# From expert sums to output with tokens on partitions, and overflow rounds ahead of the main round

## The reference

```python
# first block, after its attention: x is (256, 1024)
hx2 = modulate(rmsnorm(x, norm2_g), sh2, sc2)
x = x + g2 * moe(hx2, ...)        # 32 experts, the 4 best of each token, hidden width 1024
x = rmsnorm(x, final_g)
# second block
h = rmsnorm_2(x, norm_mix_pre)
merged = ...                       # three attentions of h @ w_in, gated and summed
x = x + rmsnorm_2(merged @ w_out, norm_mix_post)
h = rmsnorm_2(x, norm_ffn_pre)
u = causal_depthwise_conv(h @ w_ffn_up, ...)          # 2 x 2816 channels
y = (gelu(u_gate) * u_val) @ w_ffn_down
x = x + rmsnorm_2(y, norm_ffn_post)
```

## Time and profile before

| what | us |
|---|---|
| median of 3 runs | 1701.89 |
| lowest and highest of them | 1701.84, 1705.04 |
| the profiled execution's own time | 1704.64 |
| its span in the profile | 1702.8 |
| PE busy in the span | 1586.2 |
| DVE, ACT busy | 542.3, 435.3 |

### The profile page before, as it was taken

How to read it: one execution, slowest core, us unless ns; L and a number is a source line. 1 busy time by engine, 2 the same in 40 slices (tenths; PEclk the granted TensorE clock), 3 DMA queues, 4 the chain that set the end, 5 groups by cost and what they waited for, 6 DMA issues and landing times.

```text
span 1702.8 us, 23717 instructions
## 1 busy us (share of the span) xinstructions
PE 1586.2 (93%) x10016; PEld 977.8 (57%) x10016; DVE 542.3 (32%) x1089; ACT 435.3 (26%) x849; POOL 7.2 (0%) x16
## 2 busy tenths in 40 slices
PE   5999999999999999999999999998699999899997
PEld 3786776443343333334333433333299988789997
DVE  3755513110101010110101010101255474477863
ACT  3433622010001010101101100000445552456542
POOL 0000000000000000000000000000000100000000
PEclk9999998999999999999999999999999999999999
DMA  9325736999999999999999999999734624425420
GB/s 393 152 80 221 294 119 250 433 431 432 432 431 431 431 431 431 431 433 434 433 433 432 433 431 432 431 432 431 299 116 157 186 99 149 149 99 198 175 99 25
DMA packets 27432, 524.79 MB, mean 308 GB/s; under 512 B 2931, under 2 KB 7027, under 8 KB 7492
## 3 DMA queue, kind: packets, MB, share of 16 engines
q1 hardware_dynamic: 24368, 519.06, 73.2%
q10 hardware_dynamic: 2484, 3.19, 0.7%
q0 software_dynamic: 512, 1.57, 0.4%
HBM read 522.72 MB, written 1.08 MB: 308 GB/s over the span
## 4 chain that ended last, share of the span: by engine, by line
PE 59%; DMA 34%; DVE 3%; ACT 2%; issue 1%; SPq 0%; ACTq 0%; DVEq 0%
PE ps L596 58%; DMA ring<-in_w_down 33%; PE ps L724 1%; DMA arena<-in_ctxT 1%; DMA ring<-in_first 1%; DVE ring_r L1641 0%; DVE arena L1623 0%; PE ps L1078 0%; DVE nrm L1620 0%; ACT w_high L1448 0%; DVE hx_lo L1648 0%; DVE arena L1654 0%; DVE arena L1955 0%; ACT L1191 0%; ACT arena L1198 0%
## 5 line engine op out<-in xcount | busy, mean ns | idle before, releaser
L596 PE MATMUL ps<-ring,arena 128*64 128x512 f32 (+1 forms) x3872 | 721.6, 532 | 45.4 <-DMA ring<-in_w_down 31.2
L596 PEld LDWEIGHTS ps<-ring,arena 128*64 128x64 f32 (+1 forms) x3872 | 240.3, 132 | 478.1 <-issue 403.4
L596 PE MATMUL ps<-arena_r,w_high 128*128 128x256 f32 x1840 | 339.5, 287 | 10.2 <-DVE arena_r L1935 9.4
L596 PEld LDWEIGHTS ps<-arena_r,w_high 128*128 128x128 f32 x1840 | 289.8, 193 | 15.0 <-issue 12.2
L596 PE MATMUL ps<-arena 128*128 128x128 f32 (+5 forms) x1780 | 262.4, 379 | 6.8 <-DVE arena L1838 1.6
L596 PE MATMUL ps<-arena_r,ring_r 128*128 128x256 f32 x920 | 261.7, 284 | 0.0
L1862 DVE TENSOR_SCALAR arena<-ps 128x512 f32<-128x512 f32 x32 | 22.1, 692 | 716.4 <-PE ps L596 716.4
L596 PEld LDWEIGHTS ps<-arena 64*128 64x128 f32 (+3 forms) x1780 | 167.5, 176 | 112.1 <-issue 98.1
L596 PEld LDWEIGHTS ps<-arena_r,ring_r 128*128 128x128 f32 x920 | 178.2, 194 | 0.0
L1909 DVE TENSOR_TENSOR ring_r<-ring,w_high 128x1024 fp32r<-128x1024 f32 x120 | 142.0, 1221 | 102.4 <-ACT w_high L1448 102.4
L1448 ACT ACTIVATE w_high<-ring 128x1024 fp32r<-128x1024 f32 x120 | 120.8, 1054 | 26.4 <-PE ps L596 26.4
(11 more groups left out here) (203 smaller groups left out, 1052.2 us busy)
## 6 DMA issues: line engine op xcount, KB each, us to landing
ring<-in_w_gate_up SPq DMA_DIRECT2D x64, 4096.0 KB, 20.8
ring<-in_w_down SPq DMA_DIRECT2D x32, 4096.0 KB, 19.7
ring<-in_second SPq DMA_DIRECT2D x32, 2048.0 KB, 8.2
ring<-in_first SPq DMA_DIRECT2D x19, 2048.0 KB, 12.5
ring<-in_first SPq DMA_DIRECT2D x3, 1024.0 KB, 5.1
ring<-in_second SPq DMA_DIRECT2D x2, 1024.0 KB, 5.0
small<-in_small ACTq DMA_DIRECT2D x1, 1024.5 KB, 8.3
arena<-in_xT SPq DMA_DIRECT2D x1, 1024.0 KB, 8.1
```

Of the source, the lines that this page charges most:

```text
L596: return nc.tensor.matmul(out_, lhsT, rhs, start=start, stop=stop, **kw)
```

## The change

- After the experts the residual is `x_tm`: 2 groups of 128 tokens on partitions, each with 1024 features. `combine` is 4 products of 128 tokens by 512 features; the residual itself is added by 16 products with the identity (`add_residual`) ahead of the last expert's down product.
- g2 is put on a row by 2 products of ones with a diagonal, and multiplied into `b_dn` once and into each expert's output by DVE (`scaled_down`), which takes the copy from ACT.
- `start_sums` becomes 4 products of 512 columns, all ahead of the branch and the first gather.
- Overflow rounds, with their branches, stand ahead of the main round on PE, ACT, DVE and SP.
- Norms take sums along a row (ACT's Square with an accumulator). The normed residual is turned back to features by products with a diagonal of the inverse roots (`turned`), from which ACT and DVE make the high and low parts.
- Output and down products have tokens as the stationary operand (128x128) and 512 weight columns as the moving one (`token_rows`); the last four down parts are done for token group 0 first and group 1 after it.
- Three rows of norm weights (512 KB each, repeated on all partitions) are loaded on ACT's queue. The output leaves in 4 writes of 256 KB.

```diff
-            stream(moe_units, 0, slot_full)
             sp.wait_ge(most_set, 1)
             count = sp.value_load(most_i[0:1, 0:1], min_val=0, max_val=T)
             with sp.If(count > SLOTS):
...
+            stream(moe_units, 0, slot_full)
...
+            pe.wait_ge(g2_set, 1)
+            for half in range(2):
+                mm(ps[:, 4 + half, :], ones[:], g2_diag[:, 4 * half:4 * half + 4].rearrange("p k n -> p (k n)"), True,
+                   True).then_inc(g2_mm, 1)
             sum_squares(NORM2, sq2, 2, T)
...
+            for bank in (6, 7, 5, 4):
+                t, half = (bank - 4) // 2, bank % 2
+                if bank == 4:
+                    pe.wait_ge(most_set, 1)
+                mm(ps[:, bank, :], gates_t[:, P * t:P * t + P], b_dn[0:N_EXPERTS, 512 * half:512 * half + 512], True, False,
+                   skip_group_check=True)
...
-                def combine():
-                    for c in range(4):
+                def combine(done):
+                    for t in range(TT):
                         for half in range(2):
-                            m = 4 * half + c
                             rows_ = slice(SLOTS * half, SLOTS * half + SLOTS)
-                            last = mm(ps[:, 4 + m // 2, T * (m % 2):T * (m % 2) + T], y_e[rows_, P * c:P * c + P],
-                                      sgt[rows_, :], False, False, skip_group_check=True)
+                            last = mm(ps[:, 4 + 2 * t + half, :], sgt[rows_, P * t:P * t + P], y_e[rows_, :], False, False,
+                                      skip_group_check=True)
+                        if done is not None:
+                            last.then_inc(done, 1)
                     return last
...
+                def add_residual():
+                    for t in range(TT):
+                        for k in range(KC):
+                            mm(ps[:, 4 + 2 * t + k // 4, P * (k % 4):P * (k % 4) + P], xT[:, k, P * t:P * t + P], ident,
+                               False, False, skip_group_check=True)
...
+                if S is MAIN:
+                    add_residual()
                 pe.wait_ge(S.at_ready, r * 32 + N_EXPERTS)
                 pe.wait_ge(S.sgt_ready, r * 33 + (N_EXPERTS + 1))
                 filled_pair(2, N_EXPERTS)
                 down(2, 0)
                 down(2, 1)
-                combined(N_EXPERTS - 1).then_inc(S.round_done, 1)
+                if S is MAIN:
+                    combined(N_EXPERTS - 1, x2_mm)
+                else:
+                    combined(N_EXPERTS - 1).then_inc(S.round_done, 1)
...
-            round_pe(MAIN, 0, start_sums)
             with if_more(pe):
...
+            round_pe(MAIN, 0)
+            def turned(x, t, k):
+                return mm(chunk_bank(k)[:, P * t:P * t + P], x[:, t, P * k:P * k + P], diag[:, t, :], True, True)
+            pe.wait_ge(diag_set, TT)
+            for k in range(KC):
+                if k >= 4:
+                    pe.wait_ge(h_lo_set, 2 * KC + k - 3)
+                for t in range(TT):
+                    last = turned(x_tm, t, k)
+                last.then_inc(turn_mm, 1)
...
+            def token_rows(n, t, bank, hi, lo, k, first, last):
+                tok = slice(P * t, P * t + P)
+                w_hi = part_hi(n)
+                w_lo = part_of(n, ring_r)
+                for x_, w, at_start, at_end in ((hi, w_hi, first, False), (lo, w_hi, False, False), (hi, w_lo, False, last)):
+                    for half in range(2):
+                        done_ = mm(ps[:, bank + half, :], x_[:, k, tok], row_of(w, half), at_start, at_end,
+                                   skip_group_check=True)
+                return done_
+            for k in range(KC):
+                n = 2 * J_OUT + k
+                pe.wait_ge(w_lo_set, N_PARTS1 + n + 1)
+                pe.wait_ge(mg_lo_set, k // 2 + 1)
+                for t in range(TT):
+                    last = token_rows(n, t, 4 + 2 * t, x_hi, merged_lo, k, k == 0, k == KC - 1)
+                    if k == KC - 1 and t == 0:
+                        last.then_inc(mo_mm, 1)
+                last.then_inc(part_mm, 1)
+            pe.wait_ge(br_used, 12)
+            for t in range(TT):
+                pe.wait_ge(diag_set, TT + t + 1)
+                for k in range(KC):
+                    if t and k >= 4:
+                        pe.wait_ge(h_lo_set, 3 * KC + k - 3)
+                    last = turned(x_tm, t, k)
+                    if t:
+                        last.then_inc(turn_mm, 1)
...
+            for t in range(TT):
+                for f in range(FC - DOWN_TAIL, FC):
+                    if t == 0:
+                        pe.wait_ge(w_lo_set, N_PARTS1 + 2 * J_DN + f + 1)
+                        pe.wait_ge(f_lo_set, f // 2 + 1)
+                    last = down(f, t)
+                last.then_inc(y_mm, 1)
...
+            def square_tm(stage, n, src, total, scale=1.0):
+                if n:
+                    act.wait_ge(sum_set, n)
+                A(unread_tm[stage].rearrange("p (a b) -> p a b", a=2), src, ACT.Square, scale=scale,
+                  accum_out=total).then_inc(sum_set, 1)
+            def turned_hi(k, g, before):
+                act.wait_ge(turn_mm, before + k + 1)
+                A(x_hi[:, k], chunk_bank(k), ACT.Copy, scale=g[:, k:k + 1]).then_inc(h_hi_set, 1)
+            for n in range(HI_PARTS - 1):
                 split_hi_part(n)
...
+                act.wait_ge(x2_mm, t + 1)
+                square_tm("mix", t, banks_tm(4 + 2 * t), sums_mix[:, 1, t:t + 1])
+            for t in range(TT):
+                act.wait_ge(z_set, t + 1)
+                square_tm("mix", TT + t, halves(x_tm[:, t]), sums_mix[:, 0, t:t + 1])
+            act.wait_ge(ms_set, 1)
+            A(roots_mix[:], roots_mix[:], ACT.Sqrt).then_inc(root_set, 1)
+            load_table(ACT.Exp)
+            split_hi_part(HI_PARTS - 1)
...
+            act.dma_start(post_row, io["rows"][:, 1, :]).then_inc(post_in, 16)
+            act.dma_start(last_row, io["rows"][:, 2, :]).then_inc(post_in, 16)
...
+                square_tm("post", 2 * TT + t, banks_tm(4 + 2 * t), sums_post[:, t:t + 1], scale=0.5)
+                root_tm(2 * TT + t + 1, sums_post, roots_post, t, twice=1)
+            split_hi_part(2 * J_UP + 2)
+            for t in range(TT):
+                act.wait_ge(x3_set, t + 1)
+                square_tm("post", 3 * TT + t, halves(x_tm[:, t]), sums_ffn[:, t:t + 1])
+                root_tm(3 * TT + t + 1, sums_ffn, roots_ffn, t)
+            load_table(ACT.Gelu_apprx_tanh)
+            split_hi_part(2 * J_UP + 3)
...
+            dve.wait_ge(pt_mm, len(TURNS) - 2)
+            V.tensor_tensor(g2_diag, ident.unsqueeze(1).to_broadcast([P, KC, P]),
+                            modcol[:, 40:48, 0:1].to_broadcast([P, KC, P]), ALU.mult).then_inc(g2_set, 1)
...
+            dve.wait_ge(g2_mm, 2)
+            for half in range(2):
+                rows_ = slice(SLOTS * half, SLOTS * half + SLOTS)
+                V.tensor_copy(g2_rows[rows_], ps[rows_, 4 + half, :])
+            dve.wait_ge(bdn_in, 16)
+            V.tensor_tensor(b_dn[0:N_EXPERTS].rearrange("p (a b) -> p a b", a=2),
+                            b_dn[0:N_EXPERTS].rearrange("p (a b) -> p a b", a=2), ps[0:N_EXPERTS, 4:6, :], ALU.mult)
...
+                def scaled_down(e, unit):
+                    dve.wait_ge(S.units, (r * N_EXPERTS + e) * UNITS_EXPERT + (unit + S.units0))
+                    V.tensor_tensor(y_e, ps[:, 3, :], g2_rows, ALU.mult).then_inc(S.y_ready, 1)
                 next_pair(1)
                 expert(0, 2)
                 with dve.Fori(0, N_EXPERTS // 2 - 1) as i:
                     expert(i * 2 + 1, 1)
                     gated(i * 2 + 1)
                     next_pair(i + 2)
+                    scaled_down(i * 2, 5)
                     expert(i * 2 + 2, 1)
                     gated(i * 2 + 2)
+                    scaled_down(i * 2 + 1, 5)
...
+            split_lo_part(0)
+            split_lo_part(1)
+            dve.wait_ge(rows_in, 16)
+            for t in range(TT):
+                dve.wait_ge(sum_set, t + 1)
+                V.tensor_tensor(halves(x_tm[:, t]), banks_tm(4 + 2 * t), halves(final_row), ALU.mult).then_inc(z_set, 1)
+            dve.wait_ge(sum_set, 2 * TT)
+            V.tensor_scalar(roots_mix[:, 1], sums_mix[:, 1], 1.0 / D, EPS, ALU.mult, ALU.add)
+            link(V.tensor_scalar(eps_mix[:], sums_mix[:, 1], EPS / D, EPS * EPS, ALU.mult, ALU.add))
+            V.scalar_tensor_tensor(roots_mix[:, 0], sums_mix[:, 0], 1.0 / D, eps_mix[:], ALU.mult,
+                                   ALU.add).then_inc(ms_set, 1)
+            dve.wait_ge(root_set, NORM_MIX + 1)
+            link(V.reciprocal(roots_mix[:], roots_mix[:]))
+            for t in range(TT):
+                V.tensor_scalar(diag[:, t], ident, roots_mix[:, 0, t:t + 1], None, ALU.mult).then_inc(diag_set, 1)
...
+            def step_of(stage, t, bank, roots, row, done, at=slice(0, D)):
```

(13 more changed lines are left out.)

311 lines of the change are left out of this document (133 added, 178 removed).

## The result

The changed kernel takes **1679.97 us** (median of 4 runs, 1678.88 to 1680.33), against 1701.87 us (1700.76 to 1705.04, 4 runs) for the kernel before: ratio 0.987, 95% interval 0.985 to 0.988. The profiled execution took 1679.69 us, its span is 1677.9; before they were 1704.64 and 1702.8. So the spans differ by 24.9 us, the medians by 21.9.

The account below looks back on a forecast made before the run. Weight stream bounds the experts, PE the rest; gains 13.0 + 7.9 + 11.2 less costs 3.6 and 3.6 make 24.9 us: 1679.7 against the profiled execution, 1677 against the median 1701.9; range 1669 to 1690.

Parts of the forecast that it names:

- head: Before the first expert: g2's products, 1.5 us of uncovered branch and gathers with copies cost 3.6 us; bounds 2.5 and 13.9.
- pass of two experts: Expert loop: the weight stream takes 58.3 us a pass, PE has 3.6 us to spare, so nothing changes.
- residual: Last expert: 16 identity products ahead of the last down product cost 3.6 us; 0 if the pair landed late, 8 at half clock.
- norm after the experts: Last expert sum to the second block's first product: 24.3 us becomes 11.3, gain 13.0; bounds 8 and 15.
- output product and middle norms: Output product's start to the first up product: 44.1 us becomes 36.2, gain 7.9; bounds 4 and 11.
- down product: Second block: 528 products at 0.120 us plus six of ones become 264 at 0.229, 60.4 us; gain 5.6.
- end: After the last product: 13.0 us becomes 7.4, since group 0 is done under group 1's products; gain 5.6.
- then gather (16 records, 2.0 us), ACT's copy [...] gather, copy: Head, after the branch: two gathers of 2.0 us and two copies of 0.8, from 281.4 to 287.0 us.
- the branch is not covered: Rival at the head: the overflow branch stands uncovered, cost 13.9 us instead of 3.6, total 1687; chance 0.15.
- The loop's back branch: Slower rival in the expert loop: a 7.3 us fetch each pass adds 55 us, total 1732; chance 0.04.
- ScalarE's table load and split hold the first chunk: Norm after the experts: ACT's table load (1.3) and one split (1.05) hold the first chunk until 7.7 us.
- The wider product: Second block's output and down products: one 512-column product costs 0.229 us where two of 256 cost 0.240.

Follow-up runs that it names:

- run 6: Changed kernel plus three extra, overwritten 128 by 512 products on TensorE in each of 15 two-expert passes: 1680.73 us.
- run 1: The changed kernel timed once more, unedited: 1680.44 us; its profiled execution took 1677.92.
- the first group: Changed kernel, unedited and with three separate edits (guard behind main round, guard uncovered, residual moved), timed beside the kernel before, median 1701.35 us.
- run 2: Changed kernel with the guarded overflow rounds put back behind the main round on all four engines: 1680.26 us against 1680.44.
- run 3: Changed kernel with TensorE's guard and overflow branch ahead of start_sums, so no queued work covers them: 1686.43 us, 6.0 above the changed kernel.
- Run 10: Changed kernel with ScalarE, behind the experts, making the turned columns before loading the Exp table and rounding the last weight part: 1680.39 us.
- run 8: Changed kernel with the second block's 512-column output and down products issued as twice as many of 256 columns: 1684.39 us.
- run 5: Changed kernel with g2's two products moved from ahead of the second norm's squares into TensorE's wait for the gates: 1678.91 us.
- run 11: Changed kernel with residual and g2's products moved into TensorE waits and two norm orders changed, guard still ahead of the main round: 1674.29 us.
- run 12: Changed kernel with residual and g2's products moved into waits, two norm orders changed, and guard back behind the main round: 1669.65 us.

## Why the prediction was right, and where it was off

The forecast was the likeliest case, and it came: 1679.97 against 1677 in a range of 1669 to 1690, faster as said. Its terms against the two profiled executions:

| term | predicted | measured | where |
|---|---|---|---|
| head | -3.6 | -6.0 | first bias product 283.42 to 289.43 |
| pass of two experts | 0 | 0 | 58.3 us both; run 6 |
| residual | -3.6 | -3.2 | last sum's end +9.2, less 6.0 |
| norm after the experts | +13.0 | +13.8 | 24.3 to 10.6 |
| stretch up to the output product | 0 | +1.1 | starts 5.7 instead of 4.6 us earlier |
| output product and middle norms | +7.9 | +8.7 | 44.9 to 36.25 |
| down product | +5.6 | +5.0 | 191.8 to 186.8 |
| end | +5.6 | +5.5 | 13.05 to 7.5 |
| sum | 24.9 | 24.9 | spans 1702.8 and 1677.9 |

That both sums are 24.9 is luck. The head, the down product and the end were together 3.1 us worse than forecast, and the residual, the two norms and the stretch between them 3.1 us better. The 0.8 us at the middle norms come from the 1.9 us of low clock that the prediction took for the kernel before from the norm after the experts; at this place the rows have 2.7. Of the 1.1 us in that stretch, for which there was no term, 0.78 was a wait for DVE ahead of the output product, which is gone.

**The 3 us that are missing come from the base.** The prediction made the sum against the profiled execution, 1704.64 - 24.9 = 1679.7, and then subtracted it from the median, "that execution lies 2.75 us above the median of the runs, so against 1701.9 it is 1677". That would be right if what put this execution above its median stood in both. It did not: the profiled execution of the changed kernel lies on its median, and in run 1 the same kernel's lies 2.5 below. A sum of terms read in one execution carries that execution's own luck, and part of the 24.9 us was that: the medians differ by 21.9, and by 20.9 in the first group. The record shows with what this luck goes: the 23 further executions of the kernel before lie between 1699.98 us, with a mean granted clock of 0.987, and 1709.04, with 0.982; run 1 has 1677.92 with 0.988 and 1681.81 with 0.985. One place of it is the head, where the first weight product of the changed kernel comes at 291.20 here and at 289.68 in run 1. The profiled execution of the kernel before has 0.986, as others between 1700.44 and 1704.78 have, so in which term its 2.75 us lie stays open.

**The head was mis-sized**, 3.6 for 6.0, or for 4.5 in run 1 (287.91). By the rows of the execution shown: 0.6 us arise before the change's place, g2's products took 2.0 instead of 1.8, and 0.2 more came up to the first sums, which begin 1.0 later than forecast (274.19 for 271.35 + 1.8). The branch was 0.9 cheaper, 6.4 us instead of the 7.3 of the earlier trace rows, so it ended with the sums and not 1.5 behind them. The step that failed is "then gather (16 records, 2.0 us), ACT's copy [...] gather, copy": the first gather took 3.40 us, because TensorE was still at 1.2 GHz (+1.4), and the second stood still for 0.75 us in its middle, for which the trace names no releaser (+0.9 with its copy); in run 1 it did not stand still, so this part belongs to the execution. 1.0 - 0.9 + 1.4 + 0.9 = 2.4. I had the earlier trace rows before me and used the low clock for the sums only. Run 2 shows that the branch has next to no part in it: without it the first gather ended 10.87 us after the start of the sums, with it 10.80, and the first bias product came at the same time.

**The branch, the main doubt, was decided as argued.** The rival "the branch is not covered" asked for 13.9 us at the head; run 3 makes that case and has 12.2 (283.42 to 295.62), where the changed kernel has 6.0. The Trainium skill, "TensorE: Matmul & The Clock Gate", section "Architectural detail: the array is 16x 32x32, not 1x 128x128", gives TensorE a queue 64 deep; by that rule the 16 records of the sums fit, and the traces agree: 0.24 us of idle time behind 8 products and their weight loads, 8.60 with nothing queued.

**The loop's back branch stayed cheap**, as the row said: 15 of them, median 208 ns (215 before). The prediction held against it a rule on a window of two pages. The same section of the Trainium skill ("Runtime: NRT & Kernel Launch", "Instruction fetch mechanics") gives TensorE's instruction memory as 2048 instructions in another sentence; a pass of the changed kernel, 270 + 270 records, fits in that, and the 208 ns agree with it. That the overflow branch takes 5.9 to 7.3 us at either place while this one does not is shown; that the distance jumped is the reason was not tried.

**The norms** came as forecast within 0.8 us each, and their stages are most of the gain. This is read from the rows before and after; no run puts an old norm back. One term was missing: by the rows in the section on the result, about 2.2 of the 13.8 us behind the experts were the branch of before, which the prediction counted with the norm. One thing was better than forecast: I let the second block begin at the low clock, but the clock was back at 1.00 from 1230 on, while the products with the diagonal ran (0.50 from 1227 to 1229), and its first products ran at full speed (0.48 us for two instead of 0.77). Run 10 shows one step of the working wrong that happened to cost nothing: I had ScalarE's table load and split hold the first chunk, and with both moved behind the chunks the first product came at 1231.82 for 1231.93.

**The wider product** was sized right: 0.013 us per 512 columns, run 8.

## What to carry to other kernels

A long branch cost nothing where the engine had been given enough work ahead of it, and nearly its full length where it had not; whoever then makes that work faster pays the branch, as run 5 did. An addition that must be made somewhere belongs where its engine waits: the residual's 3.1 us and 1.4 us of low clock went away by moving it 15 us forward. And a prediction summed against one execution should keep that execution as its base, or widen its range by how far single executions lie from the median (here 2 to 3 us).

## What the runs showed of the hardware

**TensorE's clock did not rise under products of 32 rows.** In the changed kernel the granted clock was 0.50 in the window 275:280, in which TensorE was busy for 5.00 of 5 us with products that have 32 rows of the array in use (7.16 us for 8 records), and it was back at 1.00 in the window from 285 on, after the gather with 128 rows had run since 281.59. In run 5 the same 8 records began at the full clock and took 4.41 us; there the clock fell under them, to 0.50 from 274.0 on, while TensorE had no idle time between 271.18 and 275.59. In run 3 the clock was 0.50 through the windows from 275 to 290, the sums running from 281.62 on. But in run 2 it stayed at 0.50 under gathers with 128 rows as well, up to 288.0, and in run 1 it rose to 1.00 by 270.5, while TensorE was idle (269.95 to 271.02). No run here separates the number of rows from the products' other properties, so this is what the engine did, not a rule.

**The length of the overflow branch** varied from run to run: at the head 6.43 us in the changed kernel, 6.38 in run 1, 6.90 in run 3, 6.69 in run 5 and 6.03 in run 11; behind the experts 5.89 in run 2 and 5.96 in run 12, and 7.3 in the kernel before, which jumps over another round's code. Neither the place nor the code that is jumped over was varied by itself with enough runs to say what sets it.
